# Input projection in two float32r passes with z in channel rows, compression as mixer steps, and a new order of mixer steps

## The chip, the cores and the metric

The kernel runs on one core of a Trainium2 chip. Its time is the device time of one execution in microseconds (us). The compared figure is the median of several executions. One execution was also taken by the hardware profiler, and all stages and durations below come from that one.

## What is computed

One decoder layer over 1,024 tokens with 1,024 channels. What matters here is the first half:

```
h = rms_norm(x, norm_mix_pre)
gq, gk, gv, gz, ga, gb, nq, nkc, nvc, nks, nvs, nkw, nvw, ngate, cu = split(h @ w_in)
o_a = gated_deltanet(conv4+silu of gq,gk,gv; gate silu(gz); ga, gb)          # 6 heads of 64
o_b = native_sparse_attention(nq; nkc,nvc compressed; nks,nvs; nkw,nvw; ngate)
o_c = conformer_conv(cu)            # glu, causal depthwise conv of 31 taps, layer norm, silu
x = x + rms_norm(concat(o_a, o_b, o_c) @ w_out)
x = x + rms_norm(conv_gated_mlp(rms_norm(x)))
# compress(t): blk = 32 tokens at stride 16 + pe;  out = sum over l of blk[l] @ w[l]   (63 blocks, 2 heads)
```

`w_in` has 3,230 columns: 512 for cu, 3 x 384 for gq, gk, gv, 384 for gz, 12 for ga and gb, 384 for nq, 6 x 128 for the key and value parts, 18 for ngate.

## The kernel before, in words

Each engine runs a written-out list of its own; semaphores tie them together, and each engine takes its list in order.

**Start.** Eight tiles of 128 tokens: ScalarE takes the root mean square, VectorE scales, TensorE transposes, VectorE multiplies by the norm's gain (L1936), ScalarE makes a bf16 high part (L1891), GpSimd the low part (L2020). The products begin when all eight low parts are there.

**Input projection.** Three bf16 products for each float32 one: high x high (L2331), high x low (L2333), low x high (L2335). First come 15 units in channel rows: 128 output channels by 1,024 tokens, so 8 k-blocks x 3 products x 2 halves of 512 tokens, which is 48 products; two PSUM areas alternate. Four units are cu, nine are gq, gk, gv, two are nkc and nvc. Behind each of the nine, ScalarE takes the first tap (L2118), VectorE three more (L2245), ScalarE silu (L1895), and the rows go to DRAM (`qkv_mid`), from where the mixer reads them. VectorE also runs the 62 taps of the 31-wide convolution (L2228), both of whose tensors lie in SBUF. Then 24 token tiles (three weight blocks of 396, 512 and 402 columns, 8 tiles each), 24 products each. Weight blocks arrive through staging buffers and are split by ScalarE (L1881) and GpSimd (L1886).

**Between.** TensorE compresses keys and values (L1168: 32 float32 products each over both heads, with block-diagonal weights whose other half GpSimd sets to zero in L726), turns the conformer part back (L590), forms the cumulative gates (L1177) and goes on. GpSimd forms the low part of the conformer result (L735).

**Mixer.** 892 steps from nine threads (delta rule prepare g and scan c, sparse attention s, r, t, v, o, and w for the output weights) are merged by a string of letters, `ORDER`; every engine runs its part of each step in that order. The first prepare products are L1198, L1204, L1187, L1250, L1251, L1235; the triangular solve is L1242.

**After.** Output projection (L1552), then the MLP's up stage (L1561) and down stage (L1838), which already use two float32r products for each float32 one, and split their weights with `1 - 1/64` on ScalarE and a subtraction on GpSimd (L1626).

Of the kernel before, what the change touches and what calls it, by code (L numbers as in the profile page):

```python
# [63 lines left out]
CM_BLOCKS = [(C_CU, 512), (C_GQ, 384), (C_GK, 384), (C_GV, 384), (C_NKC, 256)]  # L64
TM_BLOCKS = [(C_GZ, GDIM + 2 * GH), (C_NKS, 512), (C_NQ, NH * HD + 3 * NH)]
CM_TILES = [(b, j) for b, (_, n) in enumerate(CM_BLOCKS) for j in range(n // P)]

# [59 lines left out]


CM_ORDER = [(0, 0), (0, 2), (0, 1), (0, 3)] + CM_TILES[4:]
CM_AFTER = [1 + max(i for i, (b, _) in enumerate(CM_ORDER) if b == n) for n in range(len(CM_BLOCKS))]  # L130
BLOCKS = CM_BLOCKS + TM_BLOCKS
NCM = len(CM_BLOCKS)
# [57 lines left out]
def ring(sizes, ends):  # L190
# [18 lines left out]
THREADS = {  # L209
    "g": sum(map(gdn_prepare, range(NT)), []),  # L210
# [9 lines left out]
    "sggsggsgsrsssgssgossgssgtssgvgssgstggssvvgstsggvssogsssosgsgsgvstsggsvvgsvsogsrtgstgsvgcsggovocsgssc"  # L220
    "gscsgccvcstgsgstvgvsstggsvcssoostggcssvvsgtvsggstsvgvvsggsssocgstgsgstvgsstgsvstsgvrvstgcsoggsogvcst"
    "vssgcgstvvsgctsggooggssccscvgtsggvsctgsvstgsgvcsvgstvggtvvgstsvggstvsgtscvosgvsvtsgrsvtsctgsgvtcsvgg"
    "ovvsogoosstsgctgsvvtggtscgscccvsggcctsvgvgstgrvvsstsggcrstsgvrrvvstsggtsgrvtggsssogvrvtgrtgrrvtgcgsv"
    "tscvggsvvostsctvstgcsvtvsvosgoostcsgvtsccgssgsvtsgvtvsggrtvgvsgstgvsrtssggrvtvgsctggvctgrvtvcsggovvr"
    "gtssgorrrgrstgcsgsvtsgvtgcsvvosgtvcsstgvcstgsvtggsvtvvgtccsggsoocggvtsvtgvssgccsgtsgvtsgvtgsvrtgsvvt"
    "cggvsrtgvrtssgrvtvgrstcrsvtvcrrvtvcstrggsvtsvggccssgosgtvsgtsccggssvogvtvggstsvtsggvvtvgsoggsoogtsvc"
    "tsgcsgsvtsgvtrgvvtgstsgrvtgcrrvtvgrvtgsgvtcssvtggcvsvstgsctgsvtgrrrvctggcsvovgtsgvgrovtcsggcsvtgsosg"
    "gvvtgstggcvvsctgscggtvsgtvgtvvgostoscwvtcvwtsvtvstvwtsvwtcvstvcvtwcvtwvtccvtcvctvwtvtwvvvoco"
# [11 lines left out]
    "qkv_st": ("prow_in", 240),  # L240
# [3 lines left out]
    "qk_in1": ("w_gate", 64),  # L244
    "wo_mm": ("cm_done", 15),
    "v_tp": ("h_tp", 8),
    "up_mm": ("tm_done", 24),
    "dn_mm": ("kT_done", 8),
    "dn_t": ("cc_tp", 8),
    "wo_hi": ("w_hi", 32),  # L250
# [4 lines left out]
    "v_ln": ("z_out", 8),  # L255
    "v_rs": ("kT_out", 8),
    "v_hi": ("h_hi", 8),
    "up_hi": ("w_hi", 40),
    "up_tap": ("tm_act", 24),
# [4 lines left out]
    "dn_hi": ("w_hi", 84),  # L264
# [3 lines left out]
    "v_hn": ("h_gained", 8),  # L268
    "v_hg": ("conv_done", 9),
    "up_c1": ("rot_mul", 16),  # L270
    "up_conv": ("cc_tok", 8),
    "f_y": ("cc_ag", 8),
    "wo_lo": ("w_lo", 32),
    "x1": ("h_lo", 8),
    "v_lo": ("rot", 32),
    "up_lo": ("w_lo", 40),
    "up_prod": ("ident_ready", 2),
    "dn_lo": ("w_lo", 84),
    "fin": ("h_lo", 16),
    "wo_st0": ("w_st0", 128),  # L280
    "wo_st1": ("w_st1", 128),
# [4 lines left out]
    "up_st2": ("w_gate", 128),  # L286
    "dn_st0": ("w_st0", 192),
    "dn_st1": ("w_st1", 192),
    "dn_st2": ("w_st2", 128),
    "dn_st3": ("w_st3", 128),  # L290
# [7 lines left out]
def build(nc, a, out, scratch, qkv_mid):  # L298
    ctx = ExitStack()
    with ctx:  # L300
# [31 lines left out]
        hT_hi = R.view(0, [KD, S], BF16)  # L332
        hT_lo = R.view(4096, [KD, S], BF16)
        wst = [R.view(8192 + 1024 * c, [2, 512]) for c in range(4)]
        wb_hi = [R.view(12288 + 4096 * s, [KD, 512], BF16) for s in range(2)]
        wb_lo = [R.view(12288 + 4096 * s + 2048, [KD, 512], BF16) for s in range(2)]
        qkvT = R.view(20480, [9, S])
        x_in = [R.view(20480 + 1024 * s, [S]) for s in range(4)]
        x_hn = [R.view(24576 + 1024 * s, [S]) for s in range(2)]
        x_hg = [R.view(26624 + 1024 * s, [KD, P]) for s in range(2)]  # L340
        zab = R.view(29696, [NT, GDIM + 2 * GH])

# [159 lines left out]
        def mix2r(name, shape):  # L502
            mix2(shape)
            return rounded(name, m2[0] - math.prod(shape), shape)
# [1914 lines left out]
```

## Time and profile before

| | us |
|---|---|
| median of 3 runs | 1378.6 (1378.44 to 1384.97) |
| profiled execution, its own time | 1376.46 |
| span of that execution | 1374.7 |
| TensorE busy in the span | 1293.8 (94%) |
| VectorE, ScalarE, GpSimd busy | 821.2, 559.8, 550.9 |
| mean granted TensorE clock | 0.987 |

The span runs from the first to the last instruction; the time holds 1.76 us more. TensorE is busy nearly throughout, so its number of products matters, and next to it the stretches in which it isn't busy. The end of a matmul is modelled and overlaps the next one's start, so the rate of products is read from their starts.

### The profile page before, as it was taken

Reading aid. Unit: us, or ns where it says so; the run is one execution under the profiler, and the core shown is the slowest. Engines: PE = TensorE matmul, PEld = TensorE weight load, DVE = VectorE, ACT = ScalarE, POOL = GpSimd, SP = SyncE. Lnnn points to the kernel's source line nnn. Section 1 sums busy time; section 2 is a strip of 40 time slices with the busy share of each in tenths; the row PEclk is TensorE's granted clock in tenths of the full one; section 3 lists DMA queues with packets and bytes.
Section 4 is the critical chain, followed back from the end, with each engine's and each line's share of the span. In section 5 each row is a group of like instructions: output and inputs, shape, how many; then the busy total and the mean of one; then the engine's idle time right before and its main releaser. Section 6 shows DMA issues by size and latency. Waiting matters only on the chain.

```text
span 1374.7 us, 23241 instructions
## 1 busy us (share of the span) xinstructions
PE 1293.8 (94%) x9669; PEld 932.8 (68%) x9697; DVE 821.2 (60%) x1104; ACT 559.8 (41%) x1005; POOL 550.9 (40%) x461
## 2 busy tenths in 40 slices
PE   4799999997999999999999799899999999999997
PEld 3344445466778777777776444588888888888775
DVE  6519997244678887979796223443333333476785
ACT  6313322114455545445455334343333333454443
POOL 3312133663233122121132424155454454496684
PEclk9999999998899999999999899999999999999999
DMA  6211332022000000000001522322222222274462
GB/s 201 80 47 62 109 96 77 1 32 50 19 19 19 4 17 19 2 19 2 2 32 32 153 78 79 105 77 77 77 67 71 77 77 65 74 248 149 145 238 77
DMA packets 90352, 98.86 MB, mean 72 GB/s; under 512 B 14348, under 2 KB 75016, under 8 KB 90248
## 3 DMA queue, kind: packets, MB, share of 16 engines
q1 hardware_dynamic: 88952, 92.65, 22.1%
q10 hardware_dynamic: 1296, 4.72, 0.9%
q8 instruction: 78, 1.28, 0.4%
q14 instruction: 26, 0.21, 0.0%
HBM read 84.20 MB, written 13.11 MB: 71 GB/s over the span
## 4 chain that ended last, share of the span: by engine, by line
PE 80%; DVE 7%; ACT 4%; issue 4%; POOL 3%; DMA 1%; SPq 0%; DVEq 0%; ACTq 0%; POOLq 0%
PE psum L1561 22%; PE psum L1838 10%; PE psum L1242 7%; PE psum L2335 6%; PE psum L2333 6%; PE psum L2331 6%; PE psum L1552 3%; PE psum L1407 3%; PE psum L1421 3%; PE psum L1391 2%; POOL arena L1511 1%; PE psum L1235 1%; PE psum L1393 1%; DVE pt_q L1154 1%; PE psum L1187 1%
## 5 line engine op out<-in xcount | busy, mean ns | idle before, releaser
L1561 PE MATMUL psum<-h_p,up_p 128*128 128x512 f32 x704 | 221.0, 390 | 2.0 <-DVE h_q L1543 1.8
L1561 PE MATMUL psum<-h_q,up_q 128*128 128x512 f32 x704 | 220.7, 389 | 0.0
L1677 DVE SCALAR_TENSOR_TENSOR arena<-psum,arena 128x1023 f32<-128x1023 f32 x44 | 56.5, 1283 | 196.1 <-ACT arena L1646 196.1
L1626 POOL TENSOR_TENSOR up_q<-arena,up_p 128x1024 fp32r<-128x1024 f32 x44 | 106.8, 2428 | 160.9 <-ACT up_p L1622 160.9
L1561 PEld LDWEIGHTS psum<-h_p,up_p 128*128 128x128 f32 x704 | 132.2, 188 | 30.2 <-DVE h_q L1543 2.3
L1561 PEld LDWEIGHTS psum<-h_q,up_q 128*128 128x128 f32 x704 | 132.2, 188 | 27.3
L2331 PE MATMUL psum<-arena 128*128 128x512 bf16 (+2 forms) x425 | 136.7, 366 | 6.2 <-POOL arena L2020 6.0
L2335 PE MATMUL psum<-arena 128*128 128x512 bf16 (+2 forms) x426 | 137.2, 366 | 0.4
L2333 PE MATMUL psum<-arena 128*128 128x512 bf16 (+2 forms) x425 | 136.8, 366 | 0.4
L1716 POOL TENSOR_TENSOR dn_q<-arena,dn_p 128x1024 fp32r<-128x1024 f32 x44 | 113.6, 2595 | 49.2 <-ACT dn_p L1712 49.2
L1732 DVE SCALAR_TENSOR_TENSOR ap_q<-ap_p,arena 128x512 fp32r<-128x512 f32 x44 | 108.5, 2492 | 37.3 <-ACT ap_p L1728 37.3
L1646 ACT ACTIVATE arena<-psum,arena 128x1024 f32<-128x1024 f32 x44 | 49.1, 1117 | 199.0 <-PE psum L1561 199.0
L1242 PE MATMUL psum<-arena 64*64 64x64 f32 x3264 | 118.6, 221 | 2.2 <-DVE arena L1038 0.9
L1242 PEld LDWEIGHTS psum<-arena 64*64 64x64 f32 x3264 | 103.6, 134 | 21.1 <-issue 9.4
L1838 PE MATMUL psum<-dn_p,ap_p 128*128 128x512 f32 x352 | 110.3, 395 | 3.8 <-DVE ap_q L1732 3.7
L1886 POOL TENSOR_TENSOR arena<-arena 128x768 bf16<-128x768 f32 (+4 forms) x28 | 53.7, 1949 | 143.7 <-ACT arena L1881 143.7
L941 ACT ACTIVATE pt_p<-psum 128x384 fp32r<-128x384 f32 x132 | 64.6, 489 | 111.8 <-PE psum L1407 111.4
L1838 PE MATMUL psum<-dn_q,ap_q 128*128 128x512 f32 x352 | 109.9, 394 | 0.0
L1154 DVE SCALAR_TENSOR_TENSOR pt_q<-pt_p,psum 128x384 fp32r<-128x384 f32 x132 | 72.9, 552 | 39.5 <-ACT pt_p L941 38.2
L2228 DVE SCALAR_TENSOR_TENSOR arena<-arena 128x1023 f32<-128x1023 f32 (+29 forms) x60 | 89.2, 1487 | 1.8
L1552 PE MATMUL psum<-arena 128*128 128x512 bf16 x376 | 84.4, 385 | 3.1 <-POOL arena L811 2.7
L935 ACT ACTIVATE arena<-psum,arena 128x640 f32<-128x640 f32 (+7 forms) x96 | 67.1, 699 | 32.2 <-DVE arena L1135 31.7
(282 smaller groups left out, 2291.0 us busy)
## 6 DMA issues: line engine op xcount, KB each, us to landing
arena<-in_ffn_w_up SPq DMA_DIRECT2D x44, 512.0 KB, 3.8
arena<-in_ffn_w_down SPq DMA_DIRECT2D x44, 512.0 KB, 3.7
arena<-in_x SPq DMA_DIRECT2D x16, 512.0 KB, 4.0
arena<-in_w_in SPq DMA_DIRECT2D x16, 384.0 KB, 3.4
qkv_mid<-arena ACTq DMA_DIRECT2D x9, 512.0 KB
arena<-qkv_mid SPq DMA_DIRECT2D x8, 576.0 KB, 4.3
arena<-in_w_in SPq DMA_DIRECT2D x8, 512.0 KB, 4.5
arena<-in_w_out SPq DMA_DIRECT2D x8, 512.0 KB, 3.7
```

Source lines behind the costliest of these rows:

```text
L1154: v.scalar_tensor_tensor(out=pt_q[x % 2], in0=pt_p[x % 2], scalar=1.0 - 1.0 / SPLIT_W, in1=psum[:, 6, 0:GDIM], op0=ALU.mult, op1=ALU.add). ...
L1242: ins = pe.matmul(out[rows, h * CH:(h + 1) * CH], lhs[rows, h], rhs[rows, h], start=start, stop=True, skip_group_check=True)
L1552: ins = pe.matmul(o, lhs[part], r[side], start=first and part == side == 0, stop=True, skip_group_check=True)
L1561: ins = pe.matmul(up_ps[j % 2][:, g, h * 512:(h + 1) * 512], w[:, k], x[:, k, h * 512:(h + 1) * 512], start=k == 0 and x is h2_p, stop=Tru ...
L1626: pool.tensor_tensor(up_q[u % 3], up_st[u % 3], up_p[u % 3], ALU.subtract).then_inc(late("up_lo")[0], 1)
L1716: pool.tensor_tensor(dn_q[kk % 4], dn_st[kk % 4], dn_p[kk % 4], ALU.subtract).then_inc(late("dn_lo")[0], 1)
L1732: v.scalar_tensor_tensor(out=ap_q[kk % 4], in0=ap_p[kk % 4], scalar=1.0 - 1.0 / SPLIT_W, in1=act_rows(kk), op0=ALU.mult, op1=ALU.add).then ...
L1838: ins = pe.matmul(dn_ps[t % HT][:, n * 512:(n + 1) * 512], x[:, tok], w[:, n * 512:(n + 1) * 512], start=first and x is ap_p[s], stop=True ...
L2228: own.up(v.scalar_tensor_tensor(out=cacc[:, c, s:S], in0=glu[:, c, 0:S - s], scalar=w, in1=cacc[:, c, s:S], op0=ALU.mult, op1=ALU.add))
L2331: pe.matmul(o, lhs[0], r_hi, start=first, stop=False)
L2333: pe.matmul(o, lhs[0], r_lo, start=False, stop=False)
L2335: ins = pe.matmul(o, lhs[1], r_hi, start=False, stop=last)
```

## The change

**The projection's arithmetic.** Each float32 product is now two float32r products: h is split into `h_p` (h/64, rounded) and `h_q` (the rest), the weights into `p` (63/64 w, rounded) and `q` (the rest), and p x h_p + q x h_q is scaled by 64 where the result is read. The products of a unit are 8 k-blocks x 2 x 2 halves, 32 in place of 48.

**The units.** 18 units in channel rows: cu, gq, gk, gv, now gz too (three units), and at the very end nkc and nvc. The token tiles are eight of 512 columns (KV) and eight of 414 columns (Q: nq, ga, gb, gates), 16 products each, on four rotating PSUM banks; before there were 24 tiles on two. The weights come in 28 pieces of up to 512 KB.

**The start.** The norm's gain is now applied with the scaling (L2285, before the transposes), ScalarE writes `h_p` and VectorE `h_q` straight from PSUM (L1996). GpSimd has no part in it. The first half (tokens 0 to 511) of units 0 and 1 is computed between the transposes of the last tiles.

**The convolution.** `glu`, the input of the 31 taps, now lies in PSUM. Taps are given out one by one: 13 in units 1 to 3, two in each of the nine conv units, 17 in the z units, one behind each token tile.

**z.** silu(gz) stays in channel rows (`zT`); VectorE multiplies it in step C2 behind the transposition, with the gain (before: GpSimd before the transposition and ScalarE behind it).

**Ring of q, k, v rows.** `y_qkv` has three buffers for the nine units (before: nine), so the first tap of unit c waits until the store of unit c-3 has landed.

**Compression.** Now mixer steps I1 and I3, head by head: 64 products with 64 contraction rows and 64 columns each for keys and for values, in place of 32 with 128 and 128. The zeroing falls away. The gates' exponentials and the layer norm's statistics run beside units 16 and 17. The letter string is new (897 steps; five `i` steps).

```diff
-CM_BLOCKS = [(C_CU, 512), (C_GQ, 384), (C_GK, 384), (C_GV, 384), (C_NKC, 256)]
-TM_BLOCKS = [(C_GZ, GDIM + 2 * GH), (C_NKS, 512), (C_NQ, NH * HD + 3 * NH)]
+CM_COLS = ([C_CU, C_CU + CCH, C_CU + P, C_CU + CCH + P] + [C_GQ + P * c for c in range(9)] + [C_GZ + P * c for c in range(3)]
+           + [C_NKC, C_NVC])
+U_CONV, U_Z, U_KC = 4, 13, 16
+TM_STEPS = ([("KV", 0), ("KV", 1)] + [x for t in range(2, NT) for x in (("KV", t), ("T", t - 2))]
+            + [("Q", 0), ("T", NT - 2), ("Q", 1), ("T", NT - 1)] + [("Q", t) for t in range(2, NT)])
+TAPS = (0, 5, 4, 4) + 9 * (2,) + (5, 6, 6)
...
 THREADS = {
+    "i": [("I0",), ("I1",), ("I2",), ("I3",), ("I4",)],
...
+            def unit(i, halves=(0, 1)):
...
+                for k in range(KD):
+                    for w, x in ((p, h_p), (q, h_q)):
+                        for h in halves:
+                            ins = pe.matmul(cm_ps[i % 2][:, h * 512:(h + 1) * 512], w[:, k], x[:, k, h * 512:(h + 1) * 512],
+                                            start=k == 0 and x is h_p, stop=True, skip_group_check=True)
...
+                if t == 4:
+                    pe.wait_ge(sem("h_lo"), 4)
+                    unit(0, (0,))
+                if t == 6:
+                    pe.wait_ge(sem("pcol_ready"), 3)
+                    unit(1, (0,))
...
+                    if c >= 3:
+                        act.wait_ge(*late("qkv_st", 16 * (c - 2)))
+                    act.activation(y_qkv[c % 3], ps, ACT.Copy,
...
+            conf_transposes(pe)
+            unit(U_KC)
+            unit(U_KC + 1)
+            conf_back(pe)
             mixer_pe(pe)
...
+            def compress(cat, w, col, load, done):
+                pe.wait_ge(sem(load), 32)
+                for kv, rows in enumerate((LO, HI)):
+                    o = psum[0:NCMP, 3, col + HD * kv:col + HD * kv + HD]
+                    for l in range(CLEN):
...
+                        ins = pe.matmul(o, lhs, w[rows, l], start=l == 0, stop=l == CLEN - 1)
```

TensorE at the start, before: all transposes (L2325; L2320 turns the parameter rows), then the bf16 products.

```order
L2325 MATMUL psum<-arena 128x128 x8
L2320 MATMUL psum<-arena 128x128 x3
L2325 MATMUL psum<-arena 128x128 x56
L2331 MATMUL psum<-arena 128x512 x2
L2333 MATMUL psum<-arena 128x512 x2
L2335 MATMUL psum<-arena 128x512 x2
```

TensorE at the same place in the changed kernel, where L2443 is a tile's eight transposes and L2428 a product of a unit: the last product of the first half of unit 0, tiles 5 and 6, then the first products of the first half of unit 1.

```order
L2428 MATMUL psum<-h_q,cm_q_54 128x512
L2443 MATMUL psum<-arena,x_hn_52 128x128 x8
L2443 MATMUL psum<-arena,x_hn_51 128x128 x8
L2428 MATMUL psum<-h_p,cm_p_55 128x512
L2428 MATMUL psum<-h_q,cm_q_56 128x512
```

Thirty-two half-width products (two lots of 16) now stand ahead of the last tiles' transposes.

TensorE from the last tile of the projection to the first mixer products, before (L564 and L590 belong to the conformer part, L1335 transposes a query tile).

```order
L2335 MATMUL psum<-arena 128x402
L564 MATMUL psum<-arena 128x128 x6
L1168 MATMUL psum<-arena 63x128 x32
L590 MATMUL psum<-arena 128x128 x16
L1168 MATMUL psum<-arena 63x128 x32
L1177 MATMUL psum<-arena 128x48 x4
L1182 MATMUL psum<-arena,kctf 128x64 x2
L1335 MATMUL psum<-arena,qsf_59 128x128 x3
L1198 MATMUL psum<-arena 128x128 x6
```

TensorE behind the last product of unit 17 in the changed kernel (L635 was L590, L1245 was L1198, L1199 was L1177, L1209 was L1168, L1223 was L1182, L1251 was L1204, L1232 was L1187, L1389 was L1335).

```order
L2428 MATMUL psum<-h_q,vc_q 128x512 x2
L635 MATMUL psum<-arena 128x128 x16
L1245 MATMUL psum<-arena 128x128 x6
L1389 MATMUL psum<-arena,qsf_89 128x128 x3
L1199 MATMUL psum<-arena 128x48 x4
L1209 MATMUL psum<-arena 63x64 x64
L1389 MATMUL psum<-arena,qsf_89 128x128 x3
L1251 MATMUL psum<-arena 128x128 x3
L1223 MATMUL psum<-arena,kctf 128x64 x2
L1209 MATMUL psum<-arena 63x64 x64
L1232 MATMUL psum<-arena 128x128 x6
```

The compression has moved behind the two last units and between the first prepare steps, and the second L1209 stands ahead of the first L1232.

GpSimd at the same place in the changed kernel: L774 to L780 are step I1 (rotation of the compressed keys), L787 the four scalings of A1b, L784 the conformer's low part (L735 before, which stood ahead of all of these), L804 the first operation of A3a.

```order
L774 MEMSET arena 128x384
L775 MEMSET arena 128x128
L779 TENSOR_TENSOR arena<-arena 63x2x32
L780 TENSOR_TENSOR arena<-arena 63x2x32
L787 TENSOR_TENSOR arena<-arena 128x384 x4
L784 TENSOR_TENSOR arena<-arena 128x2048
L804 TENSOR_TENSOR arena<-arena 128x384
```

On GpSimd the four scalings now wait behind the key rotation, and A3a behind the large subtraction.

## Rows read from the trace of the kernel before

**Rows 1.** Stages: start:end and length; busy us (instructions) per engine; clock; DMA share; GB/s

```profile
0.00:43.86 43.86, 16.37 (x68) 13.33 (x69) 30.68 (x35) 27.46 (x41) 20.24 (x21) 1.00 0.56 183
43.86:311.09 267.23, 266.23 (x1319) 132.06 (x1337) 164.14 (x174) 64.25 (x105) 99.13 (x195) 1.00 0.21 61
311.09:357.00 45.91, 35.37 (x264) 31.01 (x263) 23.43 (x50) 19.83 (x49) 18.48 (x19) 0.81 0.25 50
357.00:740.00 383.00, 372.30 (x5272) 294.65 (x5273) 309.85 (x635) 195.38 (x467) 84.98 (x93) 1.00 0.04 12
740.00:779.67 39.67, 28.25 (x207) 19.61 (x204) 19.13 (x36) 23.43 (x41) 21.84 (x13) 0.92 0.26 81
```

**Rows 2.** Chain of work inside 44 to 311 us, shares by line

```profile
by line: PE psum L2335 32.7%; PE psum L2333 32.7%; PE psum L2331 32.6%; PE psum L1945 1.3%; PE psum L564 0.4%; issue 0.4%
```

**Rows 3.** Group of ScalarE, 43.86 to 311.09 us: busy us, mean ns | idle before

```profile
L2118 ACT ACTIVATE arena<-psum,arena 128x1024 f32<-128x1024 f32 x9 | 10.0, 1114 | 67.3 <-PE psum L2335 67.3
```

**Rows 4.** Timeline of PE (start us, us) in 512-wide and 402-wide products

```profile
245.16 0.38 PE L2335 MATMUL psum<-arena 128*128 128x512 bf16 x1
...
247.75 0.38 PE L2335 MATMUL psum<-arena 128*128 128x512 bf16 x1
...
302.71 0.33 PE L2331 MATMUL psum<-arena 128*128 128x402 bf16 x1
...
303.90 0.33 PE L2333 MATMUL psum<-arena 128*128 128x402 bf16 x1
```

**Rows 5.** Chain in order of time: the up and the down stage (start us, us)

```profile
889.77 308.60 PE psum L1561 x1360
1198.37 80.66 PE psum L1838 x352
```

**Rows 6.** Timeline of PE before the first products

```profile
24.96 1.97 PE L2325 MATMUL psum<-arena 128*128 128x128 f32 x8 [1.01 <-DVE arena L2198]
...
43.86 0.63 PE L2331 MATMUL psum<-arena 128*128 128x512 bf16 x1 [5.99 <-POOL arena L2020]
...
45.99 0.76 PE L2331 MATMUL psum<-arena 128*128 128x512 bf16 x2
```

**Rows 7.** Single lines: duration ns min/median/max, first and last start, shapes

```profile
L2245 DVE SCALAR_TENSOR_TENSOR arena<-psum,arena x27: 1271/1281/1284, 98.1 to 183.5; 128x1023 f32<-128x1023 f32 x9, 128x1022 f32<-128x1022 f32 x9, 128x1021 f32<-128x1021 f32 x9
...
L2228 DVE SCALAR_TENSOR_TENSOR arena<-arena x60: 1243/1270/3026, 102.8 to 230.5; 128x1023 f32<-128x1023 f32 x2, 128x1022 f32<-128x1022 f32 x2, 128x1021 f32<-128x1021 f32 x2, 128x1020 f32<-128x1020 f32 x2
...
L1626 POOL TENSOR_TENSOR up_q<-arena,up_p x44: 2346/2408/3394, 836.9 to 1178.8; 128x1024 fp32r<-128x1024 f32 x44
...
L1561 PEld LDWEIGHTS psum<-h_p,up_p x704: 186/188/191, 873.1 to 1197.3; 128*128 128x128 f32 x176
```

**Rows 8.** Timeline, from the projection to the first mixer products

```profile
314.93 8.89 PE L1168 MATMUL psum<-arena 128*63 128x128 f32 x64 [1.58 <-issue]
...
328.08 7.26 PE L1168 MATMUL psum<-arena 128*63 128x128 f32 x64 [2.36 <-DMA arena<-in_nsa_cmp_wv]
...
330.14 4.09 POOL L735 TENSOR_TENSOR arena<-arena 128x2048 bf16<-128x2048 f32 x1 [10.66 <-ACT arena L602]
...
336.53 0.48 DVE L989 TENSOR_TENSOR arena<-psum,arena 63x128 f32<-63x128 f32 x2
...
339.18 0.31 PE L1182 MATMUL psum<-arena,kctf 64*128 64x64 f32 x2 [2.81 <-DVE kct L994]
...
347.73 1.49 PE L1187 MATMUL psum<-arena 128*128 128x128 f32 x6
...
357.00 0.92 PE L1242 MATMUL psum<-arena 64*64 64x64 f32 x24
```

**Rows 9.** DMA issues with KB each and us to landing (page, part 6; 780 to 900)

```profile
arena<-in_ffn_w_up SPq DMA_DIRECT2D x44, 512.0 KB, 3.8
...
x_mid<-arena SPq DMA_DIRECT2D x8, 512.0 KB, 2.6
```

**Rows 10.** Waits of PE in the mixer, 357 to 740 us: total, times, longest

```profile
PE psum L1407 <- DVE pt_q L1154: 2.4, 4, 1.0
```

More of the change, by code:

```diff
@@ L329, in build @@
         psum = ctx.enter_context(nc.psum_tensor("psum", [P, 8, 512], F32))
[L332 to L338, printed above, removed]
@@ L349, in build @@
+        ksf = [plain(f"ksf{s}", ks_at[s], [2 * KV, 2 * HD]) for s in range(2)]
         kT = rounded("kT", 32864, [2 * KV, S])
@@ new lines, in I1, with I2, I3 @@
+            def I1():
+                pe.wait_ge(sem("cat_out"), 4)
+                compress(kcat, wck, 0, "wck_in", "kc_mm")
+            def I2():
+                pe.wait_ge(*late("kc_lo", 1))
+                pe.wait_ge(sem("gp_exp"), 6)
+                for kv in range(KV):
+                    ins = pe.transpose(psum[:, 2, 256 + kv * CH:256 + (kv + 1) * CH], kctf[0:CH, kv], ident[0:CH, 0:CH])
+                ins.then_inc(sem("kcT_mm"), 1)
+            def I3():
+                pe.wait_ge(sem("kc_mul"), 2)
+                compress(vcat, wcv, P, "wcv_in", "vc_mm")
@@ new lines, in split_hi @@
+        def split_hi(act, n):
+            kind, c = PIECES[n]
+            act.wait_ge(sem(f"w_st{PIECE_SEM[n]}"), 16 * PIECE_USE[n])
+            if kind == "cm" and c >= 3:
+                act.wait_ge(sem("cm_done"), c - 2)
+            elif kind == "q":
+                act.wait_ge(sem("w_gate"), 32 * (1 + [k for k, _ in PIECES[:n]].count("q")))
+                act.wait_ge(*late("qkv_st", 16 * 9))
+                if c < 2:
+                    act.wait_ge(sem("w_lo"), 22)
+            elif kind == "kv":
+                act.wait_ge(sem("rope_tab"), 2)
+                act.wait_ge(sem("h_tp"), NT)
+            elif kind == "kc":
+                act.wait_ge(sem("kT_done"), NT)
+            elif kind == "vc":
+                act.wait_ge(sem("tm_done"), 2 * NT)
+            st, (p, _) = piece(n)
+            act.activation(p, st, ACT.Copy, scale=1.0 - SPLIT_W).then_inc(sem("w_hi"), 1)
@@ L2065, in _ @@
+            q_lo(pool, NT - 1)
+            for n in AFTER_Q[NT - 1]:
+                split_lo(pool, n)
             mixer_pool(pool)
@@ L2324, in _ @@
                 for k in range(KD):
[L2325 removed]
+                    ins = pe.transpose(x_ps[t % 2][:, k * P:(k + 1) * P], x_hn[t % 2][:, k * P:(k + 1) * P], ident)
                 ins.then_inc(sem("h_tp"), 1)
[L2328 to L2336 removed]
@@ L2387, in _ @@
-            for t in range(NT - 2, NT):
-                conf_transpose(pe, t)
+                if t == 4:
[4 more added lines that the diff above has]
+                    unit(1, (0,))
+            pe.wait_ge(sem("h_lo"), NT)
+            unit(0, (1,))
+            unit(1, (1,))
+            for i in range(2, U_KC):
+                unit(i)
+            for n, (name, t) in enumerate(TM_STEPS):
+                tm_free(pe, n)
+                if name == "T":
+                    kt_transpose(pe, t)
+                    continue
+                w = kv_w if name == "KV" else q_w
+                n_cols = 4 * P if name == "KV" else QCOLS
+                tok = slice(t * P, (t + 1) * P)
+                for k in range(KD):
+                    if t == 0 and k % 2 == 0:
+                        pe.wait_ge(sem("w_lo"), 1 + max(PIECES.index((name.lower(), c)) for c in range(k // 2 + 1)))
+                    for side, x in enumerate((h_p, h_q)):
+                        ins = pe.matmul(tm_bank(name, t)[:, 0:n_cols], x[:, k, tok], w[k // 2][side][:, k % 2],
+                                        start=k == 0 and x is h_p, stop=True, skip_group_check=True)
+                ins.then_inc(sem("tm_done"), 1)
```

1081 lines of the change are left out of this document (543 added, 538 removed).

## Prediction

> **What bounds the kernel now.** I read the stage table first [rows 1]. From 43.86 to 311.09 us, the input projection, TensorE is busy 266.23 of 267.23 us at clock 1.00. VectorE has 164, ScalarE 64, GpSimd 99. The chain of waits inside that stretch is 98% the three lines of bf16 products [rows 2]. So this stage is as long as its products, and fewer products shorten it until another engine is late. Ahead of it lie 43.86 us with 16.37 us of TensorE's work: it waits for the normalized, transposed x. Behind it, until the first triangular solve at 357.00, TensorE is busy 35.37 of 45.91 us at clock 0.81 [rows 1, 8]: a chain through all engines. In the mixer (357 to 740) it is busy 372.30 of 383.00 us, and its longest wait, taken over all occurrences, sums to 2.4 us [rows 1, 10]. The last 39.67 us of the mixer hold 28.25 us. Up and down stage [rows 5] aren't touched. So there are four terms: start, products, transition, mixer. The execution profiled took 1376.46 us for a span of 1374.7; the sum is made against 1376.5, which is 2.1 below the median of 1378.6.
>
> **Rates.** Starts of 512-wide bf16 products: 12 intervals in 245.16 to 247.75, so 0.2158 us each; 402-wide: 7 in 302.71 to 303.90, 0.170 [rows 4]. Before: 720 products in channel rows and 192 in token tiles at 0.2158, and 192 of 402 and 192 of 396 columns at 0.170 and 0.168, give 155.4 + 41.4 + 32.6 + 32.2 = 261.6. The stage has 267.2; 1.3 are lost at the start, where five products take 43.86 to 45.99 (0.43 each, half speed, at a granted clock of 1.00) [rows 6], and 46 transposes take the other 4.3. The model fits.
> Float32r products of 512 columns: 1360 in 308.60, 0.2269; in the down stage, where the weights are what moves, 352 in 80.66, 0.2292 [rows 5]. 414 columns aren't in the trace. From 512 to 402 columns bf16 loses 0.0458, so 98 columns are worth 0.041: 0.186.
>
> **Products.** After: 16 units before and beside the token tiles, 512 x 0.2269 = 116.2; KV 128 x 0.2292 = 29.3; Q 128 x 0.186 = 23.8; the 32 key transposes 3.0. Sum 172.3 against 265.9 (267.2 less the 1.3): **-93.6**. The last two units, 14.5, I count in the transition.
>
> **Start.** Tile 4 is transposed at 24.96 [rows 6], and its chain changes little: the gain's multiplication falls away, the split of the low part goes from GpSimd to VectorE. With the split of the first weights the first half of unit 0 starts near 27. Sixteen products, the first at half speed, take 5; tiles 5 and 6 take 2 each; the half of unit 1 takes 4; tile 7 takes 2, its two copies 2.3. The second halves start near 44.3, against a start worth 45.2 before (43.86 + 1.3), with 32 products (7.3) done: **-8.2**. What is late next is the rotation table on VectorE, ahead of ScalarE's first copy; with GpSimd idle then, it should be ready as unit 1 ends, and I price it at nothing; were it 3 us late, 3 are lost.
>
> **VectorE in a conv unit.** A unit lasts 32 x 0.2269 = 7.26 us on TensorE. Unit i waits for the conv of unit i-2. ScalarE's first tap takes 1.11 [rows 3], three taps 3 x 1.28, so conv is done 5 us after its unit: inside 7.26. With two long taps (2 x 1.27) VectorE has 6.4 of 7.26 us to do. That holds if nothing slows a tap. The row of the long taps (both inputs in SBUF) says 1270 ns in the median but 3026 at most, that of the conv taps (one input in PSUM) 1284 at most, though GpSimd worked beside both [rows 7]. `glu` is now in PSUM, so I take 1.27 for all.
> The Trainium skill, page "SBUF — State Buffer", section "Who interferes with whom", has the rule for it: a VectorE instruction with two SBUF inputs contends with a GpSimd instruction that reads SBUF, one with at most one doesn't. By it the taps cost nothing more; without it, with a split of 2.408 us [rows 7] 1.4 times a unit, a unit could take up to 9.8 us, and nine of them 22 us more. The trace agrees with the rule.
> ScalarE has 1.1 (tap) + 1.1 (silu) + 1.4 splits of about 1.1 in a unit, under 4 us; GpSimd 1.4 x 2.4 and its constants, under 6.
>
> **The ring of three rows.** ScalarE, before the first tap of unit c, waits for the store of unit c-3, which it issued one unit earlier, behind a tap, one or two splits and a silu. Queued behind that wait on ScalarE are the tap, the splits of the weights for the unit after the next, and the next silu; VectorE waits for the tap, TensorE for VectorE. From tap to tap this cycle is about 3.9 + the landing. A store of 512 KB to DRAM lands in 2.6 us where it is alone, a load in 3.8 [rows 9]: 6.5 to 7.7 against 7.26. Beside 1.4 loads a unit it is nearer the upper one. I take **+3** over the six units that wait (0.5 each), bounds 0 and 20 (landing 6.7, 3.3 late in each of six).
>
> **Transition**, from the last Q product. Last rotation, last copy: 1.9; conformer transposes 1.8, two units 14.5, transposes back 1.8: 20.0. Gate exponentials, statistics and the last splits run beside the two units; cover gone, they would cost some 13. Then ScalarE's two silus, first prepare and query transposes, gates: to 23.5. Compression of the keys: the trace records each float32 product as two. 64 records of 128 columns took 8.89 and 7.26, so 0.113 to 0.139 a record [rows 8]. Now there are 128 records of 64 columns for each. Lower bound 0.038 (0.92 / 24, the solve's 64 x 64 records, several side by side), upper 0.113. I take half the 128-column record, 0.057, as its columns halve: 7.2 each, against 8.1 before. Keys done at 30.7. Then the short steps on VectorE, GpSimd, ScalarE, VectorE and the transposes that took 336.53 to 339.5 [rows 8]: 34 to 35. Then the values: 42. The second compression stands ahead of the first L1187, which was 9.3 before the first solve (347.73 to 357.00): 51.3. GpSimd's path (scalings behind the key rotation, the subtraction of 4.09 [rows 8], then A3a) ends earlier, by about 3. Against 45.9: **+5.4**. So two units are gained inside a stretch that mostly waits, which is already in the count of the products.
> On the compression the Trainium skill speaks against the change: "TensorE: Matmul & The Clock Gate", "The mechanism" in the part on packing small matmuls, says that a weight load overlaps a running matmul only if it is for other rows of the array. Here 32 products in a row use the same 64 rows. Yet the up stage's loads, 188 ns each, lie wholly inside a spacing of 227 ns on the same 128 rows [rows 5, 7]: this trace doesn't agree with it.
>
> **Mixer.** The same products; C2's work goes from GpSimd and ScalarE to VectorE, all three with room. At the first solve three of six score steps of tile 0 are still to come: **+1.5**. The new order can win at most the waits, 10.7 and 11.4 in the two stretches [rows 1], half of which is the end's fixed ping-pong; between that and a few new waits I take 0, bounds -8 and +8.
>
> **Sum.** -93.6 - 8.2 + 3 + 5.4 + 1.5 = -91.9; 1376.5 - 91.9 = 1284.6: **1285 us**.
>
> **Rivals.**
> (a) The forecast, 1270 to 1292 by its own terms: 0.54.
> (b) The conv units are set by the ring or by VectorE: a landing near 6 us beside the loads, or slowed taps. +15 over the forecast: 1300. For it: the cycle is close to the unit. Against: the DMA share in the stage is 0.21 now and would be about twice that. 0.18.
> (c) The compression goes at 0.113 a record, no load hidden: 2 x 128 x (0.113 - 0.057) = +14: 1299. It is what the skill's rule gives. Against it the up stage. 0.13.
> (d) It goes better: records at 0.038 (-5), no ring wait (-3), order worth -6: 1271. 0.11.
> (e) Slower than before: TensorE gets gaps in every unit and is then granted 1.2 GHz, as a table of clocks shows 0.81 in the only stretch with many gaps. All 172 us at half speed cost +172: 1457. It decides from 92 us of such products on. Against: a busy stage was at 1.00 throughout [rows 1]. 0.03.
> (f) The float32r products bring nothing, since their weight loads (188 ns) aren't hidden: 0.188 + 0.213 = 0.40 each, 832 x 0.174 = +145: 1430, slower. The up stage's spacing all but excludes it. 0.01.
>
> **Numbers.** The range takes in (a), most of (b) and (c), and the upper part of (d): 1269 to 1304, 8 times in 10. About 0.5% (7 us) is what a measurement can tell from no change. Faster: (a) to (d), 0.96. Slower: (f) and most of (e), 0.03. Within 0.5%: 0.01, (e) in about half of the stage.
>
> **What would show it.** First solve near 265 us (357.0 before); first second-half product near 44; starts of projection products 0.227 apart; the Q stage's end near 214 (44.3 - 7.3 + 172.3 + 3 + 2); first taps that wait for stores by less than 1 us; all short of VectorE's taps at 1.27 to 1.28. From the first solve to the output projection again 421 to 425 us, and 595 from there to the end. Wrong would be: gaps before units 5 to 15 that together pass 8 us, a transition over 60 us, or a mixer more than 8 us off.

## The result, and the profile after

The changed kernel takes 1307.4 us (median of 4 runs, 1306.4 to 1308.5) where the kernel before took 1379.1 on the same chip (1378.4 to 1385.0): a ratio of 0.947, 95% interval 0.944 to 0.950. I had forecast 1285, with a range of 1269 to 1304. The direction and most of the gain are as forecast; 22 us are missing, and the time lies 3 us above my range. One of the four executions of run e4_old_order below took 1988.6 us at a granted clock of 0.56; its median leaves it out.

The profiled execution of the changed kernel took 1308.5 us for a span of 1306.8. The stage table of that execution, in the same columns as [rows 1], with the first second-half product (43.77), the end of the last Q product (216.66), the key compression (240.3), the first solve (283.60) and the output projection (710.95) as its bounds:

```profile
0.00:43.77 43.77, 23.11 (x99) 18.59 (x99) 23.93 (x31) 25.53 (x38) 8.69 (x15) 0.99 0.62 184
43.77:216.66 172.89, 171.94 (x768) 143.32 (x768) 137.06 (x157) 63.73 (x96) 94.02 (x188) 0.98 0.28 83
216.66:240.30 23.64, 20.45 (x114) 17.39 (x114) 16.66 (x40) 9.88 (x19) 6.68 (x9) 1.00 0.59 130
240.30:283.60 43.30, 41.00 (x342) 37.55 (x341) 7.75 (x16) 8.62 (x27) 11.00 (x11) 0.53 0.12 33
283.60:710.95 427.35, 403.23 (x5482) 316.61 (x5483) 335.82 (x684) 216.10 (x506) 98.45 (x98) 0.99 0.06 19
710.95:1306.80 595.85, 575.76 (x2560) 442.10 (x2560) 273.56 (x176) 229.47 (x304) 306.24 (x122) 0.99 0.34 108
```

The projection is what it was meant to be: TensorE busy for 171.9 of 172.9 us, other engines with room. The row that stands out is the fourth. From 240.3 to 283.6 us TensorE looks busy (41.0 of 43.3 us), yet its granted clock is 0.53, and the weight loads (PEld) are busy nearly as long as the matmuls. I had expected this stretch to end at 265.

The timeline of TensorE in the transition, which answers to [rows 8] (start us, us, line, shapes, count):

```profile
218.11 1.97 PE L613 MATMUL psum<-arena 128*128 128x128 f32 x16 [1.47 <-DVE arena L2378]
...
234.67 1.91 PE L635 MATMUL psum<-arena 128*128 128x128 f32 x16
236.41 0.82 PE L1245 MATMUL psum<-arena 128*128 128x128 f32 x6
...
240.27 14.57 PE L1209 MATMUL psum<-arena 64*63 64x64 f32 x128
...
257.87 0.47 PE L1223 MATMUL psum<-arena,kctf 64*128 64x64 f32 x2 [1.56 <-DVE kct L1018]
258.27 14.58 PE L1209 MATMUL psum<-arena 64*63 64x64 f32 x128
...
283.60 0.92 PE L1289 MATMUL psum<-arena 64*64 64x64 f32 x24 [0.33 <-DVE arena L1055]
```

L1209 is the compression. Each of the two takes 14.6 us for 128 records, 0.114 a record; I had put 7.2 us, 0.057 a record. No wait of any size is shown in it: a slow instruction stream hides inside "busy". (L635's 16 records of 128 moving columns start 0.109 us apart at clock 1.00; the number is used further down.)

The timeline at the start of the second halves, and the groups of conv taps (L2333) and long taps (L2311) on VectorE (ns min/median/max), which answer to the L2245 and L2228 rows of [rows 7]:

```profile
43.77 0.80 PE L2428 MATMUL psum<-h_p,cm_p 128*128 128x512 f32 x1 [2.37 <-DVE h_q L1996]
...
49.06 0.58 PE L2428 MATMUL psum<-h_p,cm_p 128*128 128x512 f32 x1
49.48 0.40 PE L2428 MATMUL psum<-h_q,cm_q 128*128 128x512 f32 x1
...
170.15 0.63 PE L2052 MATMUL psum<-arena,ksf 128*128 128x128 f32 x4 [0.94 <-DVE ks L2018]
```

```profile
L2333 DVE SCALAR_TENSOR_TENSOR arena<-psum,arena x27: 1279/1282/1285, 77.6 to 139.7; 128x1023 f32<-128x1023 f32 x9, 128x1022 f32<-128x1022 f32 x9, 128x1021 f32<-128x1021 f32 x9
...
L2311 DVE SCALAR_TENSOR_TENSOR arena<-psum,arena x60: 1242/1266/1284, 57.8 to 211.8; 128x1023 f32<-128x1023 f32 x2, 128x1022 f32<-128x1022 f32 x2, 128x1021 f32<-128x1021 f32 x2, 128x1020 f32<-128x1020 f32 x2
```

The first 13 products start 0.43 us apart (at half clock), the later ones 0.23. From there to the key transposes at 170 us TensorE waits for nobody. ScalarE's waits from 44 to 165 us show what the ring of three rows cost (waiting tile and line, what for, us in total, times, longest):

```profile
ACT arena L2194 <- PE psum L2428: 37.6, 9, 5.5
```

L2194 is the first tap, the instruction behind the wait for the store. All nine of its waits end with TensorE's products, none with a store: the ring cost nothing.

### The profile page after: what moved, and what is told of

The parts are those of the page before. It is cut to its first block, busy times and chain, and to the rows that moved or that the text cites. A ratio compares the mean times of both kernels' runs of the same rounds, so it can differ in the third digit from the quotient of the medians.

```text
span 1306.8 us, 22593 instructions
## 1 busy us (share of the span) xinstructions
PE 1235.5 (95%) x9361; PEld 975.5 (75%) x9361; DVE 794.8 (61%) x1102; ACT 553.3 (42%) x989; POOL 525.1 (40%) x441
## 4 chain that ended last, share of the span: by engine, by line
PE 78%; DVE 10%; ACT 5%; issue 3%; POOL 3%; DMA 1%; SPq 0%; DVEq 0%; ACTq 0%; POOLq 0%
PE psum L1615 24%; PE psum L1892 10%; PE psum L2428 9%; PE psum L1289 7%; PE psum L1606 3%; PE psum L2468 3%; PE psum L1461 3%; PE psum L1475 3%; PE psum L1445 3%; PE psum L1209 2%; DVE arena L2311 2%; DVE pt_q L1186 1%; POOL arena L1565 1%; ACT pt_p L969 1%; PE psum L1232 1%
## 5 line engine op out<-in xcount | busy, mean ns | idle before, releaser
L2428 PE MATMUL psum<-h_p,cm_p 128*128 128x512 f32 x256 | 86.1, 407 | 3.6 <-DVE h_q L1996 2.4
L2428 PE MATMUL psum<-h_q,cm_q 128*128 128x512 f32 x256 | 85.4, 404 | 0.0
L1892 PEld LDWEIGHTS psum<-dn_p,ap_p 128*128 128x128 f32 x352 | 66.4, 189 | 19.9 <-POOL dn_q L1770 5.2
L1766 ACT ACTIVATE dn_p<-arena 128x1024 fp32r<-128x1024 f32 x44 | 46.5, 1057 | 78.5 <-PE psum L1892 61.1
L1892 PEld LDWEIGHTS psum<-dn_q,ap_q 128*128 128x128 f32 x352 | 66.7, 189 | 14.7
```

Of the source, the lines that this page charges most:

```text
L1892: ins = pe.matmul(dn_ps[t % HT][:, n * 512:(n + 1) * 512], x[:, tok], w[:, n * 512:(n + 1) * 512], start=first and x is ap_p[s], stop=True ...
L2428: ins = pe.matmul(cm_ps[i % 2][:, h * 512:(h + 1) * 512], w[:, k], x[:, k, h * 512:(h + 1) * 512], start=k == 0 and x is h_p, stop=True, s ...
```

## Experiments

Three theories for a record of 0.114 us. A, half clock: a record costs its 64 moving columns, 0.057, doubled by the granted 0.50. B, load: it costs the load of its 63 weight columns, whatever the clock. C, row groups: load and product of the same rows don't overlap, which was the mechanism of my rival (c). Times below are medians; the kernel before took 1378.2 in the first group of runs, 1378.8 in the second, 1380.1 in the third.

**e1_shapes: the record by itself.** One run, 1445.1 us. Seven groups of extra products ahead of the key compression, each behind 12 full-size ones, at the end of which the granted clock was 1.00; in short (the seventh group isn't used below):

```
+ for l in range(96): pe.matmul(o[0:NCMP, 0:64], far(LO, l), wck[LO, l % 32], ...)      # L1227
+ for l in range(32): pe.matmul(o[0:NCMP, 0:128], far(LO, l), two(LO, l), ...)          # L1230
+ for l in range(32): pe.matmul(o[0:32, 0:64], far(LO, l, 32), wck[LO, l], ...)         # L1233
+ for l in range(32): pe.matmul(o[0:NCMP, 0:64], far(ALL, l), wck[:, l], ...)           # L1236
+ for l in range(32): pe.matmul(o[0:NCMP, 0:64], kcat[LO, 0, at:at + NCMP], wck[LO, l]) # L1239, contiguous
+ for l in range(32): one product on LO (L1242), one on HI rows to the other outputs (L1243)
```

> The changed kernel with seven groups of extra float32 products ahead of the key compression, each group behind 12 full-size products (128 x 128 weights, 512 columns) that keep TensorE at a granted clock of 1.00. Every product is recorded as two. Spacing of records, as (rows, weight columns, moving columns). Theory A, half clock: a record costs its moving columns, and 0.113 was measured only because the granted clock was 0.50; so (64, 63, 64) 0.057, (64, 63, 128) 0.113, (64, 32, 64) 0.057, (128, 63, 64) 0.057. Theory B, weight load: a record costs the load of its 63 weight columns at either clock: (64, 63, 64) 0.11, (64, 63, 128) 0.113 to 0.12, (64, 32, 64) near 0.057, (128, 63, 64) 0.11, and the same with contiguous weights unless their stride of 16 elements is what makes the load slow. Theory C, row groups: load and product of the same rows don't overlap: (64, 63, 128) 0.16 or more, and rows alternating between the two halves are twice as fast. If the clock falls inside the group of 96 products although it began at 1.00, a quarter of the array is too little to hold it. The kernel itself takes about 140 us longer by these groups; the output's values are unchanged.

Groups of TensorE by line and shape (rows*weight columns, moving shape, records | busy us, mean ns), and the stage table: two stretches inside the first group, one inside the alternating pair L1242 and L1243:

```profile
L1227 PE MATMUL psum<-arena 64*63 64x64 f32 x192 | 21.3, 301 | 0.0
...
L1230 PE MATMUL psum<-arena 64*63 64x128 f32 x64 | 7.2, 271 | 0.0
L1236 PE MATMUL psum<-arena 128*63 128x64 f32 x64 | 7.2, 274 | 0.0
L1242 PE MATMUL psum<-arena 64*63 64x64 f32 x64 | 7.2, 270 | 0.0
L1243 PE MATMUL psum<-arena 64*63 64x64 f32 x64 | 7.2, 270 | 0.0
L1233 PE MATMUL psum<-arena 64*32 64x64 f32 x64 | 3.9, 218 | 0.0
L1239 PE MATMUL psum<-arena 64*63 64x64 f32 x64 | 3.9, 218 | 0.0
```

```profile
254.00:257.00 3.00, 3.00 (x30) 3.00 (x29) 0.00 (x0) 0.00 (x0) 0.00 (x0) 1.00 0.00 0
262.00:265.00 3.00, 3.00 (x31) 3.00 (x29) 0.00 (x0) 0.00 (x0) 0.00 (x0) 0.50 0.00 0
...
354.00:357.00 3.00, 3.00 (x59) 3.00 (x58) 0.00 (x0) 0.00 (x0) 0.00 (x0) 1.00 0.00 0
```

Divide busy time by count. The compression's shape takes 0.111 a record at full clock, and as many records pass in 3 us at 1.00 as at 0.50. So A alone is out. Twice the moving columns cost the same; half the weight columns cost 0.061, near half; twice the rows cost the same. That is B, and it has one more condition: the same 63 columns laid one after the other (L1239) take 0.061. The spread ones stand 16 elements, 64 bytes, apart. C is out too: with contiguous loads the same rows take a product every 0.061 us, and alternating with the other half of the rows (L1242, L1243) leaves the spread ones at 0.112 per half, so there was no load time that another half's product could hide. The two halves of the array run side by side, both groups in the same 7.2 us.
The Trainium skill, "TensorE: Matmul & The Clock Gate", section "LDWEIGHTS (loading the stationary operand)", says that a load's time goes by its columns and not its rows. These rows agree, and add what the page doesn't say: spread columns cost about twice.
A second thing: the group of 96 products began at 1.00, had no gap, and its clock fell after 5 to 6 us of 64 x 64 products (0.55 between 258 and 261 us, 0.50 at 262). The groups of 7.2 us behind it, which move 128 columns, use 128 rows or alternate between the halves, kept 1.00, as did the shorter ones.

**e2_late_values: the value compression where the clock was high.** The step that issues it on TensorE is made part of the later step I4, which moves in the order:

```
-    "ggggsiisgiiigsgsgsssgssggstgsssvgvsgsstgsssvvrgs...
+    "ggggsiisgiigsgsgsssgssggstgsssvgvsgsstgisssvvrgs...
```

> The value compression moved from ahead of the first solve to a place some 25 steps later, among score steps and solves, where TensorE had been at a granted clock of 1.00. Theory A (half clock): its 128 records take 7.3 instead of 14.5 us, first solve 14 earlier, whole kernel about 7 faster (1300). Theory B or C (load): they take 14.5 there too, first solve 14 earlier, kernel within 2 us of the changed kernel's 1307.

1312.7 us, ratio to the kernel before 0.952 (0.951 to 0.954). The late step can read v after its place has been reused, so the compressed values are wrong in this run; the number and the shapes of the products are the same. Timeline and stages:

```profile
279.58 14.52 PE L1209 MATMUL psum<-arena 64*63 64x64 f32 x128
```

```profile
279.58:282.58 3.00, 3.00 (x34) 3.00 (x30) 0.90 (x2) 0.00 (x0) 0.00 (x0) 1.00 0.02 5
282.60:294.10 11.50, 11.44 (x102) 11.07 (x101) 0.00 (x0) 0.00 (x0) 0.00 (x0) 0.50 0.00 0
294.10:299.70 5.60, 4.57 (x54) 3.90 (x54) 2.32 (x6) 2.35 (x11) 0.54 (x1) 0.50 0.20 56
```

14.5 us again, as B says; and again the clock falls inside it. The work only changed its place, and brought its half clock with it, which lasts to 299.7 us over the solves behind it. The time isn't within 2 us of 1307 as I had expected of B, but 5 worse: the first solve comes 13.2 us earlier (270.36), the output projection 6.1 later (717.0). The compression accounts for 14.5 of these 19.3; the other 4.8 aren't traced to single steps.

**e3_quadrants: the two heads side by side.** Outputs of head 1 go to partitions 64 to 126, and the products alternate:

```
-                for kv, rows in enumerate((LO, HI)):
-                    o = psum[0:NCMP, 3, col + HD * kv:col + HD * kv + HD]
-                    for l in range(CLEN):
+                for l in range(CLEN):
+                    for kv, rows in enumerate((LO, HI)):
+                        o = psum[halves[kv], 3, col:col + HD]
```

(The steps behind it take the keys and values from there; positions are loaded for both halves.)

> Both key and value compression with the two heads side by side: head 0 on rows and output partitions 0 to 63, head 1 on 64 to 127, alternating product by product. Theory A (half clock): if the two run at the same time, 7 us instead of 14.5 at half clock, less if the fuller array brings the clock back. Theory B (one load after the other, 0.11 each): 14.5 again. Theory C (row groups): loads hide behind the other half's products, about 7. So A and C give about 1307 - 15 = 1292, B 1307.

1290.0 us, 0.936 (0.933 to 0.938): 17 us better than the changed kernel. Both compressions in its stage table:

```profile
240.30:247.60 7.30, 7.30 (x130) 7.22 (x130) 2.00 (x4) 2.57 (x11) 0.00 (x0) 0.77 0.23 34
250.10:257.40 7.30, 7.30 (x130) 7.22 (x130) 0.00 (x0) 1.12 (x3) 6.84 (x5) 0.77 0.15 44
```

7.3 us each, half of 14.6. Here my expectation for B was wrong: loads for different rows do run at the same time. The first solve comes at 264.84, 18.8 us earlier, of which the compressions give 14.6. The other 4.2 is the work between them and behind them, now mostly at full clock: 12 transposes (L1232, here L1228) took 3.1 us at half clock, and 1.8 here. This run has also one transpose in place of two between the compressions, a matter of 0.1 us.

**e4_old_order: the order of mixer steps of the kernel before**, with the five compression steps put in near its start.

> The changed kernel with the order of mixer steps of the kernel before; the five steps of gates and compression are put in after its sixth and seventh step group, and one weight step near the end is exchanged with the last scan step. My prediction held the new order to be worth 0 within 8 us. If the new order brought the mixer's extra 3 us (427.3 against 422.7 from first solve to output projection), the old one takes them back: about 1304. If the later C2 work on VectorE and ScalarE or the moved start of the scores did, the time stays at 1307 or gets worse. The new order may also be worth 5 or more here, since it was made for this kernel: 1312.

1312.1 us, 0.952 (0.950 to 0.954): 5 worse. First solve at 287.5 (3.9 later). From there to the output projection 425.5 us (1.9 less), TensorE busy 400.7 (2.5 less) with 5,472 records in place of 5,482. So the new order does work before the first solve differently, and what looks like a slower mixer is partly work moved into it.

**e5_contiguous: weights one after the other**, heads as they were.

```
-  out=dst[:, half].rearrange("p (n l) -> p n l", l=STRIDE),
+  out=dst[:, half].rearrange("p (l n) -> p n l", l=STRIDE),
...
-  lhs = cat[rows, l // STRIDE, l % STRIDE:l % STRIDE + STRIDE * (NCMP - 1) + 1:STRIDE] if l < STRIDE else ...
+  at_ = l % STRIDE * CH + l // STRIDE
+  lhs = cat[rows, l // STRIDE, at_:at_ + NCMP]
```

> The changed kernel with the copies of k and v that the compression reads laid out position-in-stride first, so that the 63 weight columns of every product lie one after the other instead of 16 elements apart. The shapes run measured 0.058 us a record for such weights at full clock against 0.110 for the spread ones. Load theory (the stride costs 0.05 a record): keys and values take 7.4 us each if the clock holds, 14 less in all, 1293. But a quarter of the array in use let the clock fall after some 6 us in the shapes run, and at half clock 64 moving columns should cost 2 x 0.057 = 0.114: then nearly nothing is won, and the time stays near 1305. Half-clock theory alone: no change at all.

1307.6 us, 0.947 (0.943 to 0.950): no change. The key compression:

```profile
240.40:254.70 14.30, 14.24 (x131) 13.89 (x130) 1.98 (x3) 2.60 (x11) 0.00 (x0) 0.50 0.13 18
```

14.2 us at half clock, 0.111 a record where the same record took 0.061 at clock 1.00 (e1, L1239). So the half clock alone holds it there; that it does so through the 64 moving columns fits the numbers (2 x 0.057), but no run separates them from a load that halves with the clock. Two limits of the same size lay on top of each other: at half clock contiguous weights gain nothing (here), and with spread weights full clock gains nothing (e1, e2). The loads' busy share doesn't tell them apart: it is 13.9 of 14.3 us here, too.

**e6_both: side by side and contiguous.**

> Heads side by side in two quarters of the array, and contiguous weights. Side by side alone each compression took 7.2 us (64 pairs of records at 0.11, two loads in one spacing) and the kernel 1290. With contiguous weights a pair of records costs 0.058 at full clock, 0.114 at half: each compression 3.7 us, at least at the start of a full-clock stretch, the kernel 5 to 7 faster than side by side alone: 1284. If the clock is at half from the first window on, 1290 again.

1285.3 us, 0.931 (0.927 to 0.934). Compressions of 5.5 us (from 241.15) and 3.9. The mean clock from 240 to 245 us is 0.66, so it was at half for 3.4 of these 5 us:

```profile
240.00:245.00 5.00, 5.00 (x89) 4.95 (x90) 1.98 (x3) 3.69 (x12) 0.00 (x0) 0.66 0.61 88
```

**e7_both_fill: TensorE kept busy ahead of the second halves.**

```
+  def fill(n):
+      for _ in range(n):
+          pe.matmul(psum[:, 1, 0:P], ident, ident, start=True, stop=True, ...)
...
+  if t == NT - 1:
+      fill(4)
...
+  fill(10)
   pe.wait_ge(sem("h_lo"), NT)
   unit(0, (1,))
```

> The kernel before this one with extra float32 products of the identity (128 x 128 weights, 128 columns) in TensorE's two waits ahead of the second halves of the first units: four ahead of the transposes of the last x tile (0.9 us) and ten behind them (2.3 us). Theory: the half clock of the first 13 products from 43.8 to 49.5 us comes of the waits ahead of them; kept busy TensorE stays at 1.00 and 2.7 us are won. Rival: the clock looks further back than these two waits (all of 0 to 43 is half idle), it falls all the same, and the time changes by less than 1 us.

1280.9 us, 0.929 (0.926 to 0.931), the fastest. Its stage table at the start of the second halves and in the transition, and its timeline:

```profile
44.00:50.00 6.00, 6.00 (x27) 4.83 (x26) 2.66 (x7) 3.52 (x5) 0.72 (x1) 1.00 0.00 0
236.30:255.30 19.00, 16.39 (x350) 14.23 (x347) 7.54 (x17) 9.81 (x28) 10.45 (x10) 1.00 0.35 85
```

```profile
237.28 3.90 PE L1209 MATMUL psum<-arena 64*63 64x64 f32 x128
...
243.76 3.90 PE L1209 MATMUL psum<-arena 64*63 64x64 f32 x128
...
255.33 0.86 PE L1285 MATMUL psum<-arena 64*64 64x64 f32 x22
```

The clock stays at 1.00 through both, each compression takes 3.9 us (0.030 a record) and the first solve comes at 255.3, ahead of my 265. Side by side each half takes a product every 0.061 us, what one half alone took with contiguous weights (e1, L1239): theory C, by which the other half's products would hide a load, has nothing left to explain.
The intervals of this run and of e6 overlap, so how much of the 4.4 us between them is the fillers isn't settled by the medians; the 2.7 of the first 13 products is in the profile. The compression is the same in both, with the same wait of 1.74 us ahead of it, and yet its clock fell in e6 and not here; e6's execution with the mean clock of this profile (0.991) took 1281.5 us, this one 1281.3. So the 1.00 in the transition isn't shown to come of the fillers or of the shape of the products.

**e8_two_taps: VectorE relieved.** The nine conv units leave out the tap of distance 1, so q, k and v miss that part of their convolution.

```
-                    for s in range(1, 4):
+                    for s in (2, 3):
```

> The changed kernel without the tap of distance 1 in each of the nine conv units (q, k and v then miss that part of their convolution), so VectorE has 11.6 us less to do in the projection. My prediction said that VectorE with 6.4 of 7.26 us a unit sets nothing. If so, the start of the token tiles' products stays where it is, and only waits that come from VectorE's backlog vanish: the 0.9 us ahead of the first key transposes and perhaps the 1.5 ahead of the conformer transposes; first solve 1 to 2.4 us earlier. If VectorE did set units, more than 3 us are won.

One run, 1303.1 us, first solve at 280.1, 3.5 earlier. The token tiles' products start 1.4 us earlier (156.63), for a reason that has nothing to do with taps: the second halves started 0.8 earlier, and only 8 of their products ran at half clock instead of 13. Then comes 0.9 for the wait ahead of the first key transposes, gone. The last 1.0 arises behind the value compression, where the half clock ended earlier in this run. The 1.5 ahead of the conformer transposes stayed. So VectorE's backlog cost the projection about 1 us: it sets no unit.

**e9_gap_fill: the wait ahead of the key compression filled.**

```
+  pe.wait_ge(sem("cat_out"), 4)
+  for _ in range(8):
+      pe.matmul(psum[:, 3, 0:P], ident, ident, start=True, stop=True, ...)
   pe.wait_ge(sem("cc_act"), 2)
```

> The changed kernel with eight extra float32 products of the identity (1.8 us) in TensorE's wait of 1.74 us ahead of the gates and the key compression. Rival on the clock: the waits between 234 and 240 us made it fall at 240.6; with this one filled it stays at 1.00 through the compression, the solve comes some 5 us earlier. Theory: 64 x 64 products keep a quarter of the array busy and let the clock fall by themselves, as in the group of 96 products of the shapes run, which began at full clock and lost it after 6 us; then the fall comes a few us later at most, each compression takes 14.1 to 14.6 us again, since its loads (0.110) hold at either clock, and the solve moves by less than 2 us.

One run, 1306.8 us. Its stage table:

```profile
238.60:242.40 3.80, 3.80 (x35) 3.76 (x35) 1.98 (x3) 2.44 (x11) 0.00 (x0) 1.00 0.40 58
242.40:253.20 10.80, 10.74 (x97) 10.44 (x96) 0.00 (x0) 0.00 (x0) 0.00 (x0) 0.50 0.01 2
```

The gap is gone and the clock falls all the same, 3.8 us into the 64 x 64 products; in the changed kernel it had fallen near their start (mean 0.73 from 240.27 to 241.00). The compression takes 14.6 us on either side of the fall at the same pace (35 records in 3.8, 97 in 10.8).

**e10_start_fill: the fillers of e7 in the changed kernel.**

> The changed kernel with the fillers of the last run but the compression as it was: extra identity products in the two waits ahead of the second halves of units 0 and 1. Theory: the first 13 products from 43.8 on run at 0.227 instead of 0.427 us, 2.7 us; the time falls from 1307.4 to 1304.5. Rival: the 5 us between the two kernels with and without fillers came from elsewhere, and here nothing comes.

1308.2 us, 0.948 (0.946 to 0.950): nothing. The products at the start do run at full speed:

```profile
44.00:50.00 6.00, 6.00 (x26) 4.87 (x27) 3.53 (x9) 2.60 (x4) 0.00 (x0) 1.00 0.00 0
...
238.60:282.70 44.10, 42.01 (x341) 38.34 (x340) 7.75 (x16) 8.28 (x27) 11.46 (x11) 0.50 0.13 33
282.70:288.90 6.20, 6.12 (x69) 5.05 (x71) 2.90 (x7) 2.20 (x8) 0.00 (x0) 0.50 0.00 0
```

The compression starts 1.65 us earlier, but the half clock lasts until 288.9 instead of 281.6, now over the first solves: from first solve to output projection it takes 430.6 us instead of 427.4. In this profile the gain is given back 200 us later. Why the half clock lasted longer isn't shown, and it doesn't follow from the earlier start: in e9 the compression started at the same time (238.64) and the clock was back at 1.00 by 280 us. In the profiles with the slow compression the half clock ended anywhere between 276 (e8) and 289 us.

**e11_best_old_order: e7 with the old order of steps.**

> The kernel with both changes of the compression and the start fillers (1280.9), with the order of mixer steps of the kernel before. With the changed kernel the old order cost 5 us: first solve 3.9 later, the mixer 1.9 shorter. If that holds whatever the compression takes, 1284; if the new order only helped because it had more to lay beside a slow compression, 1281 or less.

1287.6 us, 0.933 (0.931 to 0.936): 6.7 worse than e7, not the 3 that I expected. First solve at 266.28, 11.0 later; from there to the output projection 425.4 us, 3.0 less (1.9 in e4). The first compression ran in part at half clock, took 5.6 us instead of 3.9, and there was more half clock behind it (0.72 from 260 to 264 us):

```profile
238.40:245.20 6.80, 6.20 (x82) 6.07 (x83) 1.98 (x3) 3.30 (x13) 0.00 (x0) 0.50 0.20 30
```

So the new order's gain doesn't vanish with the fast compression; how much of the 6.7 is order and how much clock isn't separated.

## Why the prediction missed, step by step

- **Start, -8.2: right in its number, by luck in part.** Second halves at 43.77, forecast 44.3. The rotation table cost nothing. But I had TensorE's own list set the time. Tiles 5 and 6 took 1.7 us together instead of 4, at full clock, and the last tile's transposes at 40.31 waited 1.0 us for VectorE's scaled x (L2285); against that the first half of unit 0 took 5.9 instead of 5.
- **Products, -93.6: right in kind, some 3 us too small a cost.** Unit products run 0.232 apart, not the 0.2269 of the up stage: 466 intervals from 49.48 to 157.77 us, 2.5 us. Why isn't shown. Q's 0.1905 instead of 0.186: 0.6. KV products and key transposes: about 1.2 more.
- **Half clock at the start: missing.** I had it for the first half of unit 0 and not for the second halves: 13 products at 0.43, 2.7 us.
- **VectorE in a conv unit: right.** Taps at 1.28 us with 1.285 at most beside GpSimd, the long ones with `glu` in PSUM 1.284 at most (3.026 before, with both inputs in SBUF), as the Trainium skill has it ("SBUF — State Buffer", "Who interferes with whom"). Price of its backlog: 0.9 us, which I had at nothing.
- **Ring of three rows, +3: wrong, 0.** No first tap waited for a store. My estimate took a landing near that of a loaded queue and added half a microsecond a unit as insurance.
- The last Q product ended at 216.7, forecast 214.3.
- **Transition, +5.4: this step failed.** It took 66.9 us instead of 51.3. The sentence that failed is "I take half the 128-column record, 0.057, as its columns halve". The record before [rows 8, L1168] had 63 spread weight columns and 128 moving ones, and both cost 0.11 (spread loads 0.111 in e1, 128 moving columns 0.109 in L635); I read the price as the moving side's. The change halved the moving side and doubled the number of loads. That is 14.7 of the 15.6 us. Beneath it lay a second limit of the same size that I had priced at nothing, the half clock over the whole stretch: with contiguous loads it holds the record at 0.111, too (e5). The remainder hides two that cancel: products between and behind the compressions at half clock (some 4 us by e3), and an estimate of the short steps that was 3 too high.
- **Mixer, +1.5 and 0 for the order: 4.7.** TensorE is busy 2.7 us longer there and idle 2.0 longer. With the old order the busy time is that of before (400.7 against 400.6), and the idle time isn't less (24.7). So the busy part is work that the new order puts behind the first solve. The 2.0 of idle time aren't traced to one wait, and stay open.
- **The rest** (595.9, forecast 595): 0.9 more.
- Against the profiled execution (1308.5, 23.9 above 1284.6) the parts are: start -0.5, projection +4.9 (2.7 + 2.5 + 0.6 + 1.2 + 0.9, less the ring's 3), transition +15.6, mixer +3.2, the rest +0.9, together 24.1. The median is 1.1 below that execution. My own landmarks (265.6, 424.2, 595) made a span 2 us above the sum; that is slack, not a cause.

Of the rivals, (c) named the place, the price (0.113) and, with +14, nearly the size. Its mechanism isn't what happens: with contiguous columns the same rows take a product every 0.061 us, and no load time shows in it (e1, L1239; e7). The rule of the Trainium skill ("TensorE: Matmul & The Clock Gate", "The mechanism") fails on its "only": in these runs loads overlap products of the same rows. Its other half holds, since e3 shows loads and products of different rows going side by side. The same section also names, further up, a second case beside other row groups, a load into the background weight buffer; my prediction left it out. Rival (b) gave 1300 for reasons that cost 1 us. (e) and (f) didn't happen: the projection ran at 0.98 of the clock, and its loads were hidden. The range failed because I gave (c) 0.13 and nothing for the clock on top.

## What to carry to other kernels

A price per instruction belongs to the side that bound it. Before scaling it with a shape, ask which side that was (moving columns, weight columns, their spacing, clock), and if two sides fit the number, keep both ends: here moving columns and spread weight columns both gave 0.11. Small products that use part of the array should go side by side and with contiguous weights: side by side alone gave 17 us, contiguous alone nothing, both 22. And a stall removed early need not come out at the end: in e10's profile 1.65 us won at the start were lost again in the first solves, so follow a gain through the landmarks behind it.

## What the runs showed of the hardware

- Weights 16 float32 elements apart load at 0.110 us for 63 columns, at either clock (e1, e2) and for 64 or 128 rows (e1); contiguous ones for 64 rows in 0.061 or less at clock 1.00 (e1, L1239).
- Such loads for the two halves of the rows go at the same time: two in 0.11 us (e1, e3).
- The granted clock fell from 1.00 to 0.50 in streams of 64 x 64 products with no gap (e1 after 5 to 6 us, e9 after 3.8, e2 after 3), and was at 0.50 to the end of them. With the halves side by side it varied: 1.00 through e1's alternating group of 7.2 us and through both compressions of e7, at half for 3.4 us of each in e3, at half for 3.4 us in the first compression of e6, and in part of that of e11; e6, e7 and e11 compress in the same way.
- Where loads bind, half clock costs nothing (30 records in 3 us at 1.00, 31 at 0.50); what it costs is paid by the products around them.
